# Attention stage of a hybrid encoder block: a whole late tile ahead of the first scores, the other 58 from step 1

## The reference, cut to what matters

```python
proj = u @ w_in[i]
sb_q, sb_k, sb_v, sb_z, ml_q, ml_k, ml_v, ml_o, ml_z, ml_i, ml_f = _split_cols(proj)
...
        z = jnp.einsum('bhqd,bhkd->bhqk', qb, kb).astype(jnp.float32) * scale
        log_beta = jax.nn.log_sigmoid(z)
        log_keep = jnp.where(strict, log_beta - z, 0.0)
        after = lax.cumsum(log_keep, axis=3, reverse=True) - log_keep
        a = jnp.where(strict, jnp.exp(log_beta + after), 0.0)
        outs.append(jnp.einsum('bhqk,bhkd->bhqd', a, vb.astype(jnp.float32)))
```

## Time and profile before

| what | value |
|---|---|
| median of 3 runs | 1811.7 us (1810.7 to 1811.85) |
| span of the profiled execution, first to last instruction | 1808.6 us |
| that span against the median of the runs | 3.1 us less |
| PE, busy share of the span | 97% |
| DVE, ACT, POOL | 62%, 55%, 38% |

### The profile page before, as it was taken

The page is one execution under the profiler, slowest core; times in us unless marked ns, Lnnn a source line. Parts: engine busy times, 40 slices in busy tenths (PEclk is TensorE's granted clock), DMA queues, the critical chain, the costliest instruction groups (busy, mean ns, idle before and its releaser), DMA issues. The chain is left out here.

```text
span 1808.6 us, 28177 instructions
## 1 busy us (share of the span) xinstructions
PE 1761.9 (97%) x8972; PEld 1437.3 (79%) x8972; DVE 1119.1 (62%) x1776; ACT 991.3 (55%) x2041; POOL 680.6 (38%) x942
## 2 busy tenths in 40 slices
PE   7999999999899999999999999998999999999998
PEld 6888888878577887888878887886788888788887
DVE  5431214555479898979797979894666666533333
ACT  5431213322277787878787878784677776411111
POOL 1100000000147777777777777772234444200000
PEclk9999999999999999999999999999999999999999
DMA  6677766121394647454656453735555454422220
GB/s 199 163 192 215 232 186 186 52 87 47 126 282 131 172 144 212 135 175 135 174 171 185 135 176 127 249 118 190 169 193 159 162 189 139 162 77 79 81 82 40
DMA packets 193733, 277.05 MB, mean 153 GB/s; under 512 B 66684, under 2 KB 128380, under 8 KB 184408
## 3 DMA queue, kind: packets, MB, share of 16 engines
q1 hardware_dynamic: 190952, 265.19, 47.8%
q0 software_dynamic: 2672, 10.52, 1.7%
HBM read 187.41 MB, written 88.26 MB: 152 GB/s over the span
## 5 line engine op out<-in xcount | busy, mean ns | idle before, releaser
L975 PE MATMUL b_late<-w_split,spare 128*128 128x512 f32 x1416 | 411.4, 415 | 2.5 <-ACT b_p_out L1057 2.3
L756 POOL TENSOR_TENSOR b_a_lo<-b_aT,b_a_hi 128x512 fp32r<-128x512 f32 (+2 forms) x312 | 354.8, 1137 | 25.0
L1138 DVE TENSOR_TENSOR_SCAN b_buf<-b_y,b_buf 128x511 f32<-128x511 f32 (+2 forms) x320 | 357.9, 1118 | 9.1
L529 PE MATMUL a_po<-uT_hi,w_split 128*128 128x512 f32 x1024 | 318.6, 392 | 2.3 <-DVE w_split L397 2.3
L975 PEld LDWEIGHTS b_late<-w_split,spare 128*128 128x128 f32 x1416 | 243.4, 190 | 40.5 <-issue 4.6
L752 POOL CAST b_a_hi<-b_aT 128x512 fp32r<-128x512 f32 (+1 forms) x320 | 182.1, 569 | 179.1 <-PE b_o L949 147.6
L1148 DVE SCALAR_TENSOR_TENSOR b_buf<-b_buf,b_y 128x512 f32<-128x512 f32 (+2 forms) x320 | 187.9, 587 | 70.0 <-PE b_y L935 69.0
L529 PEld LDWEIGHTS a_po<-uT_hi,w_split 128*128 128x128 f32 x1024 | 193.0, 188 | 46.4 <-DVE w_split L397 2.7
L1034 ACT ACTIVATE b_aT<-b_turned 128x512 f32<-128x512 f32 (+1 forms) x320 | 170.3, 532 | 67.6 <-POOL b_a_lo L756 60.1
L529 PE MATMUL a_po<-uT_lo,w_split 128*128 128x512 f32 x512 | 201.6, 394 | 0.0
L1043 ACT ACTIVATE b_buf<-b_y 128x512 f32<-128x512 f32 (+2 forms) x320 | 171.3, 535 | 50.1 <-PE b_y L929 47.7
(11 more groups left out here) (244 smaller groups left out, 3359.6 us busy)
## 6 DMA issues: line engine op xcount, KB each, us to landing
spare<-u_pair SPq DMA_DIRECT2D x62, 1024.0 KB, 5.4
proj_n<-b_p_out SPq DMA_DIRECT2D x59, 256.0 KB, 5.7
c_gates<-proj_n SPq DMA_DIRECT2D x16, 768.0 KB, 4.5
w_raw<-in_w_in POOLq DMA_DIRECT2D x5, 2048.0 KB, 10.1
x_in<-in_x SPq DMA_DIRECT2D x16, 512.0 KB, 3.9
qk_hi<-stage_hi SPq DMA_DIRECT2D x32, 256.0 KB, 2.6
qk_lo<-stage_lo SPq DMA_DIRECT2D x32, 256.0 KB, 2.9
u_pair<-uT_hi SPq DMA_DIRECT2D x16, 512.0 KB, 3.7
```

What stands on the lines that cost most here:

```text
L529: mm = pe.matmul(po[t][:], w[:, k, m * P:(m + 1) * P], u[:, k, t * GROUP:(t + 1) * GROUP], start=(k == 0 and n == 0), stop=(k == KT - 1 an ...
L756: nc.gpsimd.tensor_tensor(lo[:, cols], raw, hi[:, cols].bitcast(F32), ALU.subtract).then_inc(lo_done, 1)
L975: mm = pe.matmul(late[:], u_in[f % US][:, u_part, k, :], w[:, k, :], start=(i == 0), stop=(i == PASSES - 1))
L1138: nc.vector.tensor_tensor_scan(down, y[u % YS][:, 1:keys][:, ::-1], down, b[:, keys - 1:keys], ALU.add, ALU.subtract).then_inc(log_done, 1)
```

## The change

Late tile 0 gets step 0 alone, so all its 24 passes stand there, and the other 58 tiles are spread over steps 1 to 333. In PE's step 0 these passes come ahead of the scores of unit 0, and the wait for POOL's constants comes behind those scores. On POOL the clearing of the old semaphores moves behind the constants, behind the column writes of the first 12 units, and behind the constants of the third stage, which move from step 4 ahead of the loop. The condition in `project` is written so that a step without passes would be taken.

```diff
-        late_start = [f * LATE_STEPS // TILES for f in range(TILES + 1)]
+        late_start = [0] + [1 + f * (LATE_STEPS - 1) // (TILES - 1) for f in range(TILES)]
...
         def _(pool):
-            for s in ended:
-                pool.sem_clear(s)
             nc.gpsimd.memset(ident[:], 0.0).then_inc(zeroed, 1)
...
+            for u in range(BUFS):
+                mask_end(u)
+            mlstm_constants()
+            for s in ended:
+                pool.sem_clear(s)
             for n in range(STEPS):
-                if has(n):
+                if has(n) and n >= BUFS:
                     mask_end(n)
-                if n == 4:
-                    mlstm_constants()
                 if has(n - H_LAG):
                     split(n - H_LAG)
...
-                if passes[0] == 0 and f > 0:
+                if 0 in passes and f > 0:
                     pe.wait_ge(u_loaded[f % US], 16 * (f // US) + (16 if f % US else 0))
                     until(pe, late_read, f)
...
-            pe.wait_ge(consts_ready, 3)
             for n in range(STEPS):
                 if has(n - F_LAG):
                     hide_future(n - F_LAG)
                 if has(n - T_LAG):
                     turn(n - T_LAG)
+                if n < LATE_STEPS:
+                    project(n)
                 if n == 0:
                     score(n)
-                if n < LATE_STEPS:
-                    project(n)
+                    pe.wait_ge(consts_ready, 3)
```

## The result

The changed kernel takes 1802.2 us in the median of 5 runs (1799.9 to 1805.0), the kernel before 1811.7 (1810.7 to 1811.9): a ratio of 0.995, 95% interval 0.9939 to 0.9962.

A forecast was written before the change was run, and what follows sets the result against it. PE was taken to bound the attention stage: 11.2 us lost at its start falls to 5.3, gaining 5.9, less 0.9 not coming back, so 5.0 off 1811.7 gives 1806.7 us; range for 8 in 10 1804.5 to 1810.3.

The forecast's parts named there:

- PE's idle time at the start: Start of the attention stage: PE idle until u tile 0 lands, 2.9 us instead of 7.6.
- The copy between tiles 0 and 1: With one bank, tile 1's first pass waits for ACT's copy of tile 0: PE waits 0.75 us.
- PE 1.3 us earlier once the 20 passes are done: At the end of step 4 PE has done 44 passes instead of 24 and is 1.3 us earlier.
- POOL's part: Moving the clearing of semaphores on POOL gains nothing by itself and loses nothing.
- SP's queue: Earlier tile releases put u tile 3 ahead of group 2's queries; later landings covered, waits taken as 0.
- u tile 1 just covered: Opening: u tile 1 lands at 497.5, covered by ACT's copy by 0.8 us.
- The 3.4 us at half: Opening, during tile 0's passes: the granted clock is at half speed for 3.4 us, a loss of 1.7.
- the rival's case: Opening: the clock stays at half for 5.9 us instead of 3.4, costing 1.3 more, time 1808.0; chance 0.14.
- the 4.6 us of 20 passes come back, less a fifth: Rest of the stage: lighter steps return the 4.6 us of passes run ahead, less an estimated 0.9 us.
- My bounds for the term: Loss on the passes coming back: 0 if PE sets all steps, 3.4 us if others hold three quarters.
- My three signs of being wrong: U tile 0 absent at 490.3; PE's stage waits growing by the start's gain; a DMA wait at tiles 2 to 5.
- what the stage gains the end gains: End of the attention stage: the same 6.0 us wait follows, so the stage's gain carries fully to the end.

The follow-up runs named there:

- again: The changed kernel with no edit, run and profiled a second time; 1805.0 us.
- pool_back: The changed kernel with POOL's part undone: clearing first again, third-block constants back to step 4; 1802.3 us.
- ceil: The changed kernel with each of tiles 2 to 58 beginning one step later; 1807.5 us.
- mid: The changed kernel with the start steps of tiles 2 to 58 rounded to nearest, so about half begin one step later; 1805.0 us.
- less: The changed kernel with the second of the 24 passes left out in tiles 1 to 58, so the output is not the reference's; 1791.6 us.
- less_mid: The changed kernel with the fourteenth of the 24 passes left out in tiles 1 to 58, so the output is not the reference's; 1793.4 us.
- scores_first: The changed kernel with PE's wait for constants and unit 0's scores again ahead of tile 0's 24 passes, new spread kept; 1808.1 us.
- old_ends: The changed kernel with all 24 passes of tile 0 ahead, but tiles 1 to 58 beginning at the steps of the kernel before; 1807.0 us.
- warm: The changed kernel with eight more matmuls, overwritten by the first pass, in PE's wait for tile 0; 1802.2 us.

## Why the prediction was wrong

**Right.** PE's idle time at the start: 2.9 us forecast, 3.0 and 2.9 measured. The copy between tiles 0 and 1: 0.75 forecast, 0.59 measured. PE 1.3 us earlier once the 20 passes are done: 19.67 - 18.35 = 1.3 at unit 5 in again and 1.3 in pool_back. POOL's part: nothing (pool_back). SP's queue: no wait at tiles 2 to 5. u tile 1 just covered: so it was in the changed kernel, again and pool_back, but not safely; ceil did not wait for it either, while mid, less and less_mid, whose code up to tile 1's first pass is the same, waited 1.2, 1.2 and 2.6 us. (The small loads behind the queries of group 2 are twelve and not fourteen; nothing hangs on it.)

**The clock.** The 3.4 us at half were what again and pool_back show (0.83 in 10 us from the first pass), and ceil, mid, less and less_mid too; the profiled execution had 5.8, the rival's case, at the rival's price (unit 5 at 19.59 instead of 18.35 us, 1.2). The Trainium skill, "TensorE: Matmul & The Clock Gate", Part 1, says that what watches the engine is free-running, so the point of change differs from run to run; the two profiles of one kernel agree, after idle stretches of 3.0 and 2.9 us. The row that the forecast took the 3.4 us from varies as well: behind the same gap of 2.25 us in the first block the clock fell in eleven of the fourteen executions and stayed up in three (last section).

**The step that failed** is the one where the 4.6 us of 20 passes come back, less a fifth: 3.7 us forecast, 6.3 measured. As far as the runs show, the fifth was not the error: taken alone a pass was worth 0.76 to 0.79 of its length (less, less_mid), and with ceil's ends the 19 passes between unit 5 and unit 319 gave 3.7 us. What I left out is that the new spread moves the ends of 53 of the 59 tiles, and with them the waits for the bank, the turns and the carries. I took those waits as given, 2.3 us and shorter, and asked only whether others would hold the lighter steps. That the places count is shown by ceil and mid. How the 6.3 us divide is an estimate: at 0.77 of their 4.4 us the 19 passes give 3.4 and the ends 2.9; if the passes come back in full, the ends give 1.9. The listed waits between unit 5 and unit 319 fall by 0.9 us (9.4 to 8.5). PE's busy time there falls by 5.5 us (708.0 to 702.5), 1.1 more than the 19 passes; what that is stays open (waits shorter than the overlap of two records do not show as idle time). My bounds for the term, 0 to 3.4 us lost, had no gain in them, so the range's low end was too high by what the ends could give. My three signs of being wrong watched only for losses, and none of them came (u tile 0 was there 2.9 and 3.0 us behind block 1).

**The second step** is that what the stage gains the end gains. The wait at the next block is the same (6.0 before, 5.9 after), but the two blocks behind it are 0.9 to 1.1 us shorter, as the clock stayed up in a gap where it fell before (5.0 and 4.6 us at half instead of 6.8). With 1.3 + 6.4 + 1.1 - 0.1 the sum is 8.7 us, against 9.5 and 6.9 us between the medians in the two sets of runs (1811.7 - 1802.2 and 1811.9 - 1805.0).

**The two halves.** The spread alone shortens the stage by 1.4 us (scores_first: 766.4 against 767.8), running ahead alone by 4.3 (old_ends), both by 7.5 (again; 6.2 in the first profile, where the clock stayed down longer). They help each other: the idle start holds 20 passes at little cost, and only the new spread takes them out of steps where they come back.

## What to carry to other kernels

Work moved into an idle start comes back where it is taken out, so take it from steps that PE sets, not from the steps right behind the start, where the next transfer waits. When a schedule is spread anew, price the count by a measured value per item, and keep a separate term of either sign for the places: three spreads with equal counts differed by 2.7 us here. For a change of half a per cent, cut the profile at a few fixed instructions and compare stretch by stretch: the stretch that repeats to 0.1 or 0.2 us shows what the kernel does, and one that does not has first to be read for the clock (and here for a transfer that came late in some executions).

## What the runs showed of the hardware

At full granted clock the first block ran at two speeds in the same code. From 396 to 476 us the profiled execution of the changed kernel made 345 matmuls, again and the twelve others 351. The two in turn:

```profile
396.00:476.00 80.00, 80.00 (x345) 63.97 (x344) 43.50 (x77) 21.12 (x37) 0.00 (x0) 1.00 0.12 46
```

```profile
396.00:476.00 80.00, 80.00 (x351) 64.22 (x350) 44.77 (x79) 21.13 (x37) 0.00 (x0) 1.00 0.13 49
```

That is 1.7%, enough for the 1.4 us by which its block 1 ended later than again's. Records can be missing, but the starts say the same: three matmuls of 512 columns that follow each other take 0.70 us there (starts 396.17, 396.87, 397.57) and 0.685 in again (396.25, 396.93, 397.62), 0.233 and 0.228 us each. Why is open.

Behind one and the same gap of 2.25 us in the first block, which no edit touched, the clock fell in eleven executions and stayed up in three. Windows of again, where it fell, and of pool_back, where it did not:

```profile
386.00:394.00 8.00, 6.11 (x20) 4.86 (x21) 3.58 (x7) 1.70 (x3) 0.88 (x1) 0.79 0.61 209
```

```profile
386.00:394.00 8.00, 6.73 (x29) 5.56 (x30) 3.58 (x7) 1.24 (x3) 0.88 (x1) 1.00 0.68 246
```

In the three (pool_back, warm, less) block 1 ended at 485.4 to 485.5 us, in the others at 486.7 to 489.1. So a median of few runs also holds how often this gap cost its 3.4 us at half speed.
